# First turns of four layers: the second token half's last two weight blocks multiplied tile by tile

## The chip, the cores and the metric

The kernel runs on one core of one Trainium2 chip. The metric is the device time of one execution in microseconds (us), the median of several runs; lower is better. The engines are PE (TensorE: matmuls and, beside them, loads of its stationary operand), DVE (VectorE), ACT (ScalarE), POOL (GpSimd) and SP (SyncE, here the issuer of most DMAs).

## What is computed

Two models in a row on 512 tokens of width 1024, all in float32. The first is one block: modulated layer norm, a joint projection, two kinds of attention (a forgetting one and a banded one), a gated merge, an output projection, a layer norm, then a feed-forward part. The second puts 16 meta tokens in front (528 tokens) and has two layers: latent attention with a feed-forward part, and a pooling mixer with a feed-forward part. The feed-forward part, which occurs three times, is the one that matters here:

```python
def conv_ffn(h, w_up, conv_w, conv_b, w_down):
    u = h @ w_up                       # 1024 -> 2 * 2816
    up = pad(u, 2 positions in front)
    u = conv_b + sum(conv_w[j] * up[:, j:j + L] for j in range(3))
    gate, val = split(u, 2)
    return (silu(gate) * val) @ w_down
```

The projections named below are up_a (feed-forward part of the first model, 512 tokens), dqkv (the first projection of the latent attention), up_b and up_c (feed-forward parts of the second model's two layers, 528 tokens).

## The kernel before, in words

**Products.** The hardware's fast float32 format keeps fewer bits than float32, so every projection is the sum of three products. A weight block w_raw (128 partitions x 1024) is rounded to w_hi by ACT (`upper`, L1699; the copy itself is L1697), and POOL makes w_lo = w_raw - w_hi (L1513). The layer's input is likewise kept as H_hi (ACT) and H_lo (DVE, L2806 in up_a and dqkv, L2967 in up_b and up_c). `mm3` (L752, matmul at L757) issues w_lo x H_hi, w_hi x H_lo and w_hi x H_hi.

**Turns.** A layer's output is made in turns (11 in each up layer) of four tiles of 128 rows; tile m accumulates in PSUM bank m. The sum runs over eight input tiles of 128 rows, two in each of the turn's four weight blocks (numbers 0 to 3 here; the next turn's are 4 to 7). So a block holds eight 128 x 128 weight tiles: two input tiles by four output tiles. `batch` (L765) runs a turn block by block, and in each block tile by tile.

**First turns in halves.** The layer's input is finished in two token halves, so the first turn of up_a, dqkv, up_b and up_c is run by `head1` (L1195, up_a and dqkv) or `head` (L1282, up_b and up_c) in halves too: first all four blocks for the first half of the tokens, then all four for the second half (256 columns), each by `half_block` (L1081). One half is 4 blocks x 4 tiles x 2 input tiles x 3 products = 96 matmuls. `h_wait` lets PE wait for each input tile of the half as it is first read.

**Signals.** `full` counts finished output tiles 0 to 2 of a turn; it is told as each gets its last product in block 3. `w_used` counts used-up weight blocks; it starts at 4 (the ring has four slots) and is told at the end of each block, in a halved turn in the second half. Tile 3 is told by the last block's w_used. `free[m]` is told when bank m has been read out; PE waits for it before the next turn's first product of tile m (`begin`, L761).

**ACT's program.** ACT works strictly through its own list. In `stage` (L1716) the rounding of coming blocks stands ahead of the reading out of the turn: in the first turn of an up layer, `upper` for blocks 5 and 6 (block 4 is done earlier), then `take` (L1987), then `upper` for block 7. `upper` of block n waits at L1706 until w_used has reached n + 1, that is until block n - 4 has been used up. `take` waits for tile m (`full`, or w_used for tile 3), writes scaled PSUM to `work` (L1994) for the four tiles, then does the silus (L2001) and rounds the products to mid_hi. DVE adds the two other taps of the convolution from PSUM (L2861): first tap of tile 0, first tap of tile 1, second tap of tile 0 (which tells free[0]), second tap of tile 1, and the same for tiles 2 and 3. In up_a and up_b blocks 0 to 3 have a place of their own (up_w_hi and up_w_lo in the trace), but the wait at L1706 for blocks 4 and up is the same.

In dqkv nothing of `take` exists: DVE copies the tiles out (L3061), while ACT rounds blocks 4 to 7 and then squares the copies (L2201) for a norm whose sums PE makes at L815 after block 4. POOL's list follows ACT's roundings (it waits for each), and SP loads a raw block into a slot once POOL has split the one before (`load_w` waits for w_lo_ok).

Of the kernel before, what the change touches and what calls it, by code (L numbers as in the profile page):

```python
# [20 lines left out]
S2 = S1 + META  # L21
# [14 lines left out]
RING = 4  # L36
# [17 lines left out]
BLK0, _n = {}, 0  # L54
# [72 lines left out]
COL2 = 512 - HALF2  # L127
# [26 lines left out]
def program(nc, xT, meta, stream, ada, vecs, consts, rel, rope, yT):  # L154
    with ExitStack() as ctx:
        def sb(name, cols, dt=F32):
            return ctx.enter_context(nc.sbuf_tensor(name, [P, cols], dt))
# [7 lines left out]
        def sem(name):  # L165
            return ctx.enter_context(nc.semaphore(name))
# [4 lines left out]
        w_hi = sb("w_hi", RING * BLK, F32R)  # L171
        w_lo = sb("w_lo", RING * BLK, F32R)
# [59 lines left out]
        own_room = {"up_a": (up1_w_hi, up1_w_lo), "up_b": (up_w_hi, up_w_lo)}  # L232
        z_all, band_w = region(("z_all", 5 * D, F32), ("band_w", 4 * P, F32))
        (_, bands) = region(("over_mid", 2 * KF * S2, F32), ("bands", 3 * BAND, F32))
        PS = ctx.enter_context(nc.psum_tensor("PS", [P, 4, 2 * 512], F32))
# [5 lines left out]
        w_used = sem("w_used")  # L241
        full = sem("full")
# [53 lines left out]
        def halves(name):  # L296
            return sem(name + "_a"), sem(name + "_b")
# [6 lines left out]
        th_ok, hi_ok, hh_ok = halves("th_ok"), halves("hi_ok"), halves("hh_ok")  # L304
# [13 lines left out]
        def ht(t, k, n=S1):  # L318
            return t[:, k * S2:k * S2 + n]

        def half(s, name=None):
            return max(HALVES[s][0], FIRST.get(name, 0)), HALVES[s][1]
# [17 lines left out]
        def tok1(t, k, s, j):  # L340
            return h1(t, k, s)[:, j * P:(j + 1) * P]
# [21 lines left out]
        def tile1(l, s, k):  # L363

            return 2 * KD * l + KD * s + k + 1
# [6 lines left out]
        def taken1(l, s, i):  # L372

            return (2 + (1 - l)) * s + 6 * l + (i // 2 if l else i - 1)
# [28 lines left out]
        def wait_y1(eng, name, s, k):  # L403

            if k < 4:
                wait_out(eng, name, 0, k, 0)
            elif s == 0:
                eng.wait_ge(y1_a, 4 * NORMS1[name] + k - 3)
            else:
                wait_out(eng, name, 0, k - 4, 1)  # L410
# [56 lines left out]
        def wtile(t, slot, kk, m, cols=4):  # L467
            o = slot * BLK + (kk * cols + m) * P
            return t[:, o:o + P]
# [274 lines left out]
        def _(pe):  # L744
# [7 lines left out]
            def mm3(out, w_h, w_l, x_h, x_l, cuts, start, stop):  # L752

                last = None
                for i, (w, x) in enumerate(((w_l, x_h), (w_h, x_l), (w_h, x_h))):
                    for a, b, c0 in cuts:
                        last = pe.matmul(out[:, c0 + a:c0 + b], w, x[:, a:b], start=start and i == 0,  # L757
                                         stop=stop and i == 2)
                return last

            def begin(name, batch, i, g):  # L761

                pe.wait_ge(free[(BATCH[name][batch][2] + i) % 4], free_before(name, batch, i, g) + 1)
# [55 lines left out]
            def hx(T):  # L819
                return lambda k: (ht(H_hi, k, T), ht(H_lo, k, T))  # L820
# [212 lines left out]
            with pe.Fori(0, 2) as g:  # L1033

                for b in range(4):
                    slot = (BLK0["v"] + b) % RING
                    pe.wait_ge(w_lo_ok, g * 4 + (BLK0["v"] + b + 1 + RING))
                    for t in range(4):
                        if b == 0:
                            begin("v", 0, t, g)  # L1040
                        for k in range(2):
                            kt = b * 2 + k
                            wr = slice(slot * BLK + k * 512, slot * BLK + k * 512 + 512)
                            hs = slice(kt * S2 + t * P, kt * S2 + t * P + P)
                            for j, (l, r) in enumerate(((H_lo, w_hi), (H_hi, w_lo), (H_hi, w_hi))):
                                last = pe.matmul(PS[:, t, 0:512], l[:, hs], r[:, wr],  # L1046
                                                 start=kt == 0 and j == 0, stop=kt == 7 and j == 2)
# [30 lines left out]
            def w_ready(n):  # L1078
                pe.wait_ge(w_lo_ok, n + 1 + RING)

            def half_block(name, b, s, rows, k0, x, start, stop, begin_tile=None, told=0, teller=None, h_wait=None,  # L1081
# [20 lines left out]
                        aside(m)  # L1102
                return last

            def sums_y(name, s, k0, k1):

                l = NORMS1[name]
                for k in range(k0, k1):
                    if k == 0:
                        wait_y1(pe, name, s, 4)  # L1110
                    wait_y1(pe, name, s, k)
                    for j in range(2):
                        o, w = 512 * s + WIDE1 * j, 64 * l + 8 * k
                        last = pe.matmul(PS[:, 0, o:o + WIDE1], tok1(X, k, s, j), lnw[:, w:w + WIDE1],  # L1114
                                         start=k == 0 and j == 0, stop=k == KD - 1, skip_group_check=True)
                if k1 == KD:
                    last.then_inc(stat1_ok[s], 1)

            def sums_squares(name, s, k0, k1):

                l = NORMS1[name]
                for k in range(k0, k1):
                    pe.wait_ge(sq1_ok, tile1(l, s, k))
                    for j in range(2):
                        o, w = 512 * s + 2 * WIDE1 + WIDE1 * j, 64 * l + 8 * k + 4
                        last = pe.matmul(PS[:, 0, o:o + WIDE1], tok1(sqx, k, s, j), lnw[:, w:w + WIDE1],  # L1126
                                         start=False, stop=k == KD - 1, skip_group_check=True)
                if k1 == KD:
                    last.then_inc(stat1_ok[s], 1)

            def spread(name, s, i):

                l = NORMS1[name]
                pe.wait_ge(dg1_ok, 2 * value1(l, s, i))
                pe.matmul(spread1(i, s), ones[:, :], diag1(i, s), start=True, stop=True).then_inc(row1_ok, 1)
# [6 lines left out]
            def spread_last(name, s):  # L1142
                if name == "out":
                    spread(name, s, 3)
                spread(name, s, 4)
# [49 lines left out]
            def head1(name, before, x, cuts=None):  # L1195

                l = NORMS1[before]

                def beside(b, m):
                    if b == 1 and m == 3:  # L1200
                        sums_squares(before, 1, 0, 4)
                    elif b == 2 and m == 1:
                        sums_squares(before, 1, 4, KD)
                    elif b == 3 and m == 2:
                        spread(before, 1, 2)
                for s in range(2):
                    def begin_tile(m):
                        pe.wait_ge(rc1_ok, taken1(l, s, 4))
                        if s:
                            begin(name, 0, m, 0)  # L1210

                    def h_wait(k):
                        pe.wait_ge(hh1_ok, tile1(l, s, k))
                    for b in range(4):
                        last = half_block(name, b, s, 2, 2 * b, x, b == 0, b == 3,
                                          begin_tile=begin_tile if b == 0 else None, told=3 * (s == 1 and b == 3),
                                          teller=full, h_wait=h_wait, cuts=None if cuts is None else [cuts[s]],
                                          aside=None if s else (lambda m: beside(b, m)))
                        if s:
                            last.then_inc(w_used, 1)  # L1220
                    if s == 0:
                        spread_last(before, 1)

# [57 lines left out]

            def head(name, before, s, h_base):  # L1282

                for b in range(4):
                    def begin_tile(m):
                        if s == 0:
                            bank_free(before, m, 0)
                        else:
                            begin(name, 0, m, 0)

                    def h_wait(k):
                        pe.wait_ge(hh_ok[s], h_base + k + 1)
                    last = half_block(name, b, s, 2, 2 * b, hx(S2), b == 0, b == 3,
                                      begin_tile=begin_tile if b == 0 else None, told=3 * (s == 1 and b == 3),
                                      teller=full, h_wait=h_wait)
                    if s == 0 and b == 2:
                        sum_x_squares(before, 1)
                    if s:
                        last.then_inc(w_used, 1)

            def pool_rows(i, k):

# [118 lines left out]
            for g in range(2):  # L1421
                for b in range(4):
# [6 lines left out]
                    for j in range(2):  # L1429
                        m = (2 * b + j) % 4  # L1430
# [4 lines left out]
                        for k in range(3):  # L1435

                            pe.wait_ge(h_ok, KD + k + 1)
                            xh, xl = cx(0)(k)
                            last = mm3(PS[:, m, :], wtile(w_hi, slot, k, j, 2), wtile(w_lo, slot, k, j, 2),
                                       xh, xl, spans(S2), k == 0, k == 2)  # L1440
                        last.then_inc(full if j == 0 else w_used, 1)
            pe.wait_ge(h_ok, KD + 5)
            for b in range(2):
                slot = (BLK0["uk"] + b) % RING
                pe.wait_ge(w_lo_ok, BLK0["uk"] + b + 1 + RING)
                for m in range(4):
                    begin("uk", b, m, 0)
                    for k in range(2):
                        xh, xl = cx(3)(k)
                        last = mm3(PS[:, m, :], wtile(w_hi, slot, k, m), wtile(w_lo, slot, k, m),  # L1450
                                   xh, xl, spans(S2), k == 0, k == 1)
# [3 lines left out]
            for b in range(2):  # L1455
                slot = (BLK0["uv"] + b) % RING
                pe.wait_ge(w_lo_ok, BLK0["uv"] + b + 1 + RING)
                for t in range(5):
                    begin("uv", b, t, 0)
                    t0 = KEYS2[t][0]  # L1460
                    for k in range(2):
                        wr = slice(slot * BLK + k * 512, slot * BLK + k * 512 + 512)
                        cs = slice((3 + k) * S2 + t0, (3 + k) * S2 + t0 + P)
                        for j, (l, r) in enumerate(((c_lo, w_hi), (c_hi, w_lo), (c_hi, w_hi))):
                            last = pe.matmul(PS[:, t % 4, 0:512], l[:, cs], r[:, wr],  # L1465
                                             start=k == 0 and j == 0, stop=k == 1 and j == 2)
# [1835 lines left out]
```

## Time and profile before

| | us |
|---|---|
| median of three runs | 2075.13 (2072.96 to 2076.39) |
| the profiled execution | 2074.31 |
| its span | 2072.5 |
| PE busy with matmuls | 2001.7 (97% of the span) |
| DVE busy | 863.9 (42%) |
| ACT busy | 836.6 (40%) |
| POOL busy | 837.1 (40%) |

The span runs from the first to the last instruction that the hardware profiler recorded; the execution's own time is a little longer. All windows and starts below are in us from the span's start. PE's busy share counts a matmul until its modelled end, and the shares of the others are averages over stages that differ. TensorE has two clock levels, 1.2 and 2.4 GHz; the profile gives the granted clock as a share of the higher one.

### The profile page before, as it was taken

What the parts mean: (1) busy time and instruction counts of PE and PEld (TensorE: products, weight loads), DVE (VectorE), ACT (ScalarE), POOL (GpSimd) and SP (SyncE); (2) the same over time, 40 slices, a digit from 0 to 9 for tenths busy, and PEclk for the clock granted to TensorE, in tenths of its full rate; (3) what the DMA queues carried; (4) which work ended last, traced back from release to release, by engine and by line L of the source; (5) the groups of instructions that cost most, each with busy time, mean ns of one, the idle gap of its engine ahead of it and who ended that gap; (6) DMA issues with size and microseconds to landing.
All of it is one profiled execution on the core that took longest, in us unless ns stands there. A gap on an engine that the chain in (4) does not pass through costs nothing.

```text
span 2072.5 us, 35722 instructions
## 1 busy us (share of the span) xinstructions
PE 2001.7 (97%) x13502; PEld 1807.8 (87%) x13506; DVE 863.9 (42%) x1607; ACT 836.6 (40%) x1347; POOL 837.1 (40%) x512
## 2 busy tenths in 40 slices
PE   7999999998999999989999989999999989999997
PEld 5887888888877778979777889999999879999997
DVE  6874540127443340166477274333400663343103
ACT  3124432334544342245577444433422553444322
POOL 1446424450534444324555523444443234434441
PEclk9999999999999999999999999999999999999999
DMA  9742002330322323213200212222232112222321
GB/s 361 278 144 92 17 16 92 96 116 12 102 91 82 102 97 105 72 54 111 72 1 1 67 36 91 81 97 94 84 101 82 62 32 101 91 91 81 112 92 51
DMA packets 54957, 184.47 MB, mean 89 GB/s; under 512 B 6992, under 2 KB 10320, under 8 KB 54864
## 3 DMA queue, kind: packets, MB, share of 16 engines
q1 hardware_dynamic: 53024, 180.97, 26.0%
q10 hardware_dynamic: 1840, 2.19, 0.3%
q8 instruction: 68, 1.11, 0.2%
q14 instruction: 25, 0.20, 0.0%
HBM read 181.03 MB, written 2.10 MB: 88 GB/s over the span
## 4 chain that ended last, share of the span: by engine, by line
PE 87%; DVE 8%; issue 2%; ACT 2%; POOL 1%; DMA 1%; DVEq 0%; ACTq 0%; SPq 0%; POOLq 0%
PE PS L757 70%; PE PS L1046 2%; PE PS L874 2%; PE PS L953 2%; PE PS L838 1%; DVE ada_acc L2396 1%; PE PS L922 1%; DVE work L2861 1%; PE PS L1002 1%; PE PS L865 1%; DVE work L2945 1%; PE PS L1114 1%; PE PS L1126 1%; PE PS L1465 1%; DVE work L2625 1%
## 5 line engine op out<-in xcount | busy, mean ns | idle before, releaser
L1513 POOL TENSOR_TENSOR w_lo<-w_raw,w_hi 128x1024 fp32r<-128x1024 f32 x263 | 637.5, 2430 | 946.8 <-ACT w_hi L1697 946.5
L1697 ACT ACTIVATE w_hi<-w_raw 128x1024 fp32r<-128x1024 f32 (+2 forms) x303 | 291.6, 981 | 715.8 <-PE PS L757 661.4
L757 PE MATMUL PS<-H_hi,w_lo 128*128 128x272 f32 (+3 forms) x2024 | 541.0, 320 | 16.7 <-DVE H_lo L2806 5.6
L757 PE MATMUL PS<-H_lo,w_hi 128*128 128x272 f32 (+3 forms) x2024 | 534.9, 317 | 0.0
L757 PE MATMUL PS<-H_hi,w_hi 128*128 128x272 f32 (+3 forms) x2024 | 533.9, 316 | 0.0
L757 PEld LDWEIGHTS PS<-H_hi,w_lo 128*128 128x128 f32 x2024 | 337.6, 189 | 54.3 <-DVE work L2861 12.9
L2861 DVE SCALAR_TENSOR_TENSOR work<-PS,vec,work 128x512 f32<-128x512 f32 (+4 forms) x264 | 186.9, 751 | 442.9 <-ACT work L1994 433.3
L757 PEld LDWEIGHTS PS<-H_hi,w_hi 128*128 128x128 f32 x2024 | 338.4, 190 | 25.8
L757 PEld LDWEIGHTS PS<-H_lo,w_hi 128*128 128x128 f32 x2024 | 338.1, 190 | 24.7
L757 PE MATMUL PS<-mid_hi,w_lo 128*128 128x256 f32 (+2 forms) x968 | 228.3, 293 | 0.0
L757 PE MATMUL PS<-mid_hi,w_hi 128*128 128x256 f32 (+2 forms) x968 | 226.9, 292 | 0.0
L757 PE MATMUL PS<-mid_lo,w_hi 128*128 128x256 f32 (+2 forms) x968 | 226.6, 292 | 0.0
L757 PEld LDWEIGHTS PS<-mid_hi,w_lo 128*128 128x128 f32 x968 | 158.1, 188 | 4.6 <-issue 0.3
L757 PEld LDWEIGHTS PS<-mid_hi,w_hi 128*128 128x128 f32 x968 | 158.2, 188 | 3.9
L757 PEld LDWEIGHTS PS<-mid_lo,w_hi 128*128 128x128 f32 x968 | 158.0, 188 | 4.0
L1994 ACT ACTIVATE work<-PS,vec 128x512 f32<-128x512 f32 (+1 forms) x132 | 102.5, 784 | 73.3 <-PE PS L757 73.3
L2929 DVE TENSOR_SCALAR work<-PS 128x256 f32<-128x256 f32 (+1 forms) x12 | 5.2, 430 | 132.8 <-ACT work L1810 132.8
L953 PE MATMUL PS<-PT,V 128*128 128x272 f32 (+1 forms) x192 | 54.8, 383 | 5.2 <-DVE work L2625 4.3
L2001 ACT ACTIVATE work<-work 128x512 f32<-128x512 f32 (+1 forms) x66 | 41.7, 632 | 45.0 <-DVE work L2861 45.0
L2396 DVE SCALAR_TENSOR_TENSOR ada_acc<-ada_w,cond,ada_acc 128x1024 f32<-128x1024 f32 x32 | 57.4, 1794 | 1.4
L2921 DVE TENSOR_TENSOR RS<-work 128x528 f32<-128x528 f32 (+1 forms) x3 | 2.1, 703 | 134.1 <-ACT work L1778 134.1
L1522 POOL TENSOR_TENSOR w_lo<-w_raw,w_hi 128x256 fp32r<-128x256 f32 x32 | 24.2, 794 | 74.4 <-ACT w_hi L1697 74.4
(369 smaller groups left out, 2961.0 us busy)
## 6 DMA issues: line engine op xcount, KB each, us to landing
w_raw<-stream SPq DMA_DIRECT2D x289, 512.0 KB, 3.3
ada_w<-ada SPq DMA_DIRECT2D x48, 512.0 KB, 5.4
X<-xT SPq DMA_DIRECT2D x8, 256.0 KB, 5.4
yT<-X SPq DMA_DIRECT2D x16, 128.0 KB, 1.7
rel_raw<-rel ACTq DMA_DIRECT2D x4, 256.0 KB, 2.8
vec<-vecs ACTq DMA_DIRECT2D x1, 390.0 KB, 3.7
sin_t<-rope ACTq DMA_DIRECT2D x1, 264.0 KB, 2.8
cos_t<-rope ACTq DMA_DIRECT2D x1, 132.0 KB, 2.5
```

What stands on the lines that cost most here:

```text
L757: last = pe.matmul(out[:, c0 + a:c0 + b], w, x[:, a:b], start=start and i == 0, stop=stop and i == 2)
L838: pe.matmul(scores1(n, par)[:, 0:w], l[rows, qs], r[rows, 0:w], start=j == 0, stop=False, skip_group_check=True)
L874: last = pe.matmul(o_psum1(par), pt_part1(n, par)[:, j * QB:(j + 1) * QB], v_head1(p, par, j), start=j == 0, stop=j == i, skip_group_check ...
L953: return pe.matmul(o_psum2(par, late)[:, a - a0:b - a0], v_weights2(p, par, j), pt2(par, j, a, b), start=j == 0, stop=stop, skip_group_che ...
L1046: last = pe.matmul(PS[:, t, 0:512], l[:, hs], r[:, wr], start=kt == 0 and j == 0, stop=kt == 7 and j == 2)
L1513: gp.tensor_tensor(w_lo[:, o], w_raw[:, o], w_hi[:, o].bitcast(F32), ALU.subtract)\
L1522: ins = gp.tensor_tensor(w_lo[:, o], w_raw[:, o], w_hi[:, o].bitcast(F32), ALU.subtract)
L1697: return act_.activation(out, in_, ACT.Copy, scale=scale)
L1994: act_.activation(ht(work, m, T)[:, a:], u(m)[:, a:], ACT.Identity, bias=v1("conv", g * 16 + (c + 3)), scale=v1("conv", g * 16 + (c + 2)))\
L2001: act_.activation(y, y, ACT.Silu).then_inc(s_ok, 1)
L2396: ins = v.scalar_tensor_tensor(a, w, cond[:, k:k + 1], a, ALU.mult, ALU.add)
L2861: ins = v.scalar_tensor_tensor(y[:, b:], u[:, b - s:T - s], w, y[:, b:], ALU.mult, ALU.add)
```

## The change

In the second token half, blocks 0 and 1 are run as before, block by block. Blocks 2 and 3 are run by the new `last_pair`: it waits for both blocks first, then takes output tile 0 through block 2 and block 3, then tile 1, and so on. `full` is told after each of tiles 0 to 2. The two w_used signals are both told in tile 3: that of block 2 when tile 3 has had its products of block 2, that of block 3 at the very end. The input tiles 4 to 7 are waited for in tile 0. The first half is unchanged, and so are the lists of ACT, DVE, POOL and SP.

```diff
--- before.py
+++ after.py
@@ -1102,6 +1102,29 @@
                         aside(m)
                 return last
 
+            def last_pair(name, s, k0, x, h_wait, cuts=None):
+
+                h_w, l_w, at = [], [], []
+                for b in (2, 3):
+                    h, l = own_room[name] if name in own_room else (w_hi, w_lo)
+                    h_w.append(h)
+                    l_w.append(l)
+                    at.append((BLK0[name] + b) % RING)
+                    w_ready(BLK0[name] + b)
+                for m in range(4):
+                    for i in range(2):
+                        for k in range(2):
+                            kt = k0 + 2 * i + k
+                            if m == 0:
+                                h_wait(kt)
+                            xh, xl = x(kt)
+                            last = mm3(PS[:, m, :], wtile(h_w[i], at[i], k, m), wtile(l_w[i], at[i], k, m), xh, xl,
+                                       [(*half(s, name), COL2)] if cuts is None else cuts, False, i == 1 and k == 1)
+                        if m == 3:
+                            last.then_inc(w_used, 1)
+                    if m < 3:
+                        last.then_inc(full, 1)
+
             def sums_y(name, s, k0, k1):
 
                 l = NORMS1[name]
@@ -1211,13 +1234,15 @@
 
                     def h_wait(k):
                         pe.wait_ge(hh1_ok, tile1(l, s, k))
-                    for b in range(4):
+                    for b in range(2 if s else 4):
                         last = half_block(name, b, s, 2, 2 * b, x, b == 0, b == 3,
-                                          begin_tile=begin_tile if b == 0 else None, told=3 * (s == 1 and b == 3),
-                                          teller=full, h_wait=h_wait, cuts=None if cuts is None else [cuts[s]],
+                                          begin_tile=begin_tile if b == 0 else None,
+                                          h_wait=h_wait, cuts=None if cuts is None else [cuts[s]],
                                           aside=None if s else (lambda m: beside(b, m)))
                         if s:
                             last.then_inc(w_used, 1)
+                    if s:
+                        last_pair(name, s, 4, x, h_wait, None if cuts is None else [cuts[s]])
                     if s == 0:
                         spread_last(before, 1)
 
@@ -1281,22 +1306,24 @@
 
             def head(name, before, s, h_base):
 
-                for b in range(4):
+                def h_wait(k):
+                    pe.wait_ge(hh_ok[s], h_base + k + 1)
+
+                for b in range(2 if s else 4):
                     def begin_tile(m):
                         if s == 0:
                             bank_free(before, m, 0)
                         else:
                             begin(name, 0, m, 0)
 
-                    def h_wait(k):
-                        pe.wait_ge(hh_ok[s], h_base + k + 1)
                     last = half_block(name, b, s, 2, 2 * b, hx(S2), b == 0, b == 3,
-                                      begin_tile=begin_tile if b == 0 else None, told=3 * (s == 1 and b == 3),
-                                      teller=full, h_wait=h_wait)
+                                      begin_tile=begin_tile if b == 0 else None, h_wait=h_wait)
                     if s == 0 and b == 2:
                         sum_x_squares(before, 1)
                     if s:
                         last.then_inc(w_used, 1)
+                if s:
+                    last_pair(name, s, 4, hx(S2), h_wait)
 
             def pool_rows(i, k):
```

## Rows read from the trace of the kernel before

**Rows 1.** The page: the span, and part 4, the chain that ended last.
```profile
span 2072.5 us, 35722 instructions
...
PE 87%; DVE 8%; issue 2%; ACT 2%; POOL 1%; DMA 1%; DVEq 0%; ACTq 0%; SPq 0%; POOLq 0%
```

**Rows 2.** Waits of PE, whole run: total us, times, longest us.
```profile
PE PS L757 <- DVE H_lo L2806: 9.3, 7, 2.9
PE PS L757 <- DVE H_lo L2967: 8.7, 10, 3.2
...
PE PS L757 <- DVE work L2861: 4.4, 3, 1.6
```

**Rows 3.** Timeline of PE, second turns of up_a, up_b, up_c: start us, us, [idle before].
```profile
527.11 0.51 PE L757 MATMUL PS<-H_hi,w_lo 128*128 128x512 f32 x1 [1.29 <-DVE work L2861]
...
1243.51 0.51 PE L757 MATMUL PS<-H_hi,w_lo 128*128 128x272 f32 x2 [1.60 <-DVE work L2861]
...
1699.71 0.50 PE L757 MATMUL PS<-H_hi,w_lo 128*128 128x258 f32 x2 [1.54 <-DVE work L2861]
```

**Rows 4.** Timeline of ACT, then the chain: up_a, end of the first turn.
```profile
520.27 1.04 ACT L1697 ACTIVATE w_hi<-w_raw 128x1024 fp32r<-128x1024 f32 x1
523.09 1.06 ACT L1697 ACTIVATE w_hi<-w_raw 128x1024 fp32r<-128x1024 f32 x1 [1.78 <-PE PS L757]
524.06 2.77 ACT L1994 ACTIVATE work<-PS,vec 128x512 f32<-128x512 f32 x4
...
524.86 1.43 DVE work L2861 x2
...
526.31 0.76 DVE work L2861
```

**Rows 5.** Timeline of ACT: up_b, end of the first turn.
```profile
1239.19 1.06 ACT L1697 ACTIVATE w_hi<-w_raw 128x1024 fp32r<-128x1024 f32 x1 [1.76 <-PE PS L757]
```

**Rows 6.** Timeline of DVE and POOL: input tiles 6 and 7 in up_a, up_b, up_c.
```profile
519.45 1.79 DVE L2806 TENSOR_TENSOR H_lo<-work,H_hi 128x256 fp32r<-128x256 f32 x1 [1.49 <-ACT H_hi L1697]
...
521.17 0.41 DVE L2806 TENSOR_TENSOR H_lo<-work,H_hi 128x256 fp32r<-128x256 f32 x1
...
1234.95 2.43 DVE L2967 TENSOR_TENSOR H_lo<-work,H_hi 128x256 fp32r<-128x256 f32 x1 [0.35 <-ACT H_hi L1697]
...
1234.69 2.41 POOL L1513 TENSOR_TENSOR w_lo<-w_raw,w_hi 128x1024 fp32r<-128x1024 f32 x1 [9.87 <-ACT w_hi L1697]
...
1691.21 2.43 DVE L2967 TENSOR_TENSOR H_lo<-work,H_hi 128x256 fp32r<-128x256 f32 x1 [0.35 <-ACT H_hi L1697]
```

**Rows 7.** Windows of PE: us, us busy (instructions), granted clock, DMA share, GB/s.
```profile
513.40:516.80 3.40, 3.40 (x18) 0.50 0.00 0
...
896.50:902.50 6.00, 6.00 (x26) 0.50 0.27 87
...
957.30:959.30 2.00, 0.00 (x1) 1.00 0.00 0
...
1663.30:1666.50 3.20, 0.04 (x1) 1.00 0.00 0
...
1243.50:1250.00 6.50, 6.49 (x53) 1.00 0.22 81
```

**Rows 8.** dqkv: timelines of DVE, PE and ACT, then the chain.
```profile
925.59 0.42 DVE L2806 TENSOR_TENSOR H_lo<-work,H_hi 128x256 fp32r<-128x256 f32 x1 [0.15 <-ACT H_hi L1697]
...
932.54 0.28 PE L757 MATMUL PS<-H_hi,w_hi 128*128 128x256 f32 x1
...
930.10 1.12 ACT L1697 ACTIVATE w_hi<-w_raw 128x288 fp32r<-128x288 f32 x4 [0.67 <-PE PS L757]
932.91 1.12 ACT L1697 ACTIVATE w_hi<-w_raw 128x288 fp32r<-128x288 f32 x4 [1.69 <-PE PS L757]
933.95 1.70 ACT L2201 ACTIVATE work<-Q 128x528 f32<-128x528 f32 x3
...
938.69 2.68 PE PS L815 x12
```

## The prediction

> **What bounds the kernel now.** I read the page first: the span and the chain that ended last. PE carries 87% of that chain, most of it one line, L757, the three-product matmul of all projections [rows 1]. A change that only reorders matmuls can gain or lose only where PE stands still, so the next view is who PE waited for. Two kinds of wait touch the changed code: for H_lo, the low half of the layer's input, at the head of a layer (L2806 in up_a and dqkv, L2967 in up_b and up_c), and three waits of 4.4 us together for L2861, the convolution on DVE that frees a PSUM bank [rows 2]. The matmul rows show where these three are: each at the first matmul of the second turn of up_a, up_b and up_c, 1.29, 1.60 and 1.54 us [rows 3]. In no other of the turns between does PE wait, so what is lost at these three places reaches the end of the kernel whole.
>
> Then what holds such a wait up, for up_a. ACT rounds weight block 6 (w_hi) from 523.09 and starts taking tile 0 out of PSUM (L1994) at 524.06; DVE starts its first L2861 at 524.86, and the third of these, from 526.31 on, frees bank 0 and lets PE go on at 527.11 [rows 3, 4]. It is one serial string, and its first link is the rounding of block 6. ACT's program says why: in the first turn `stage` puts `upper` of blocks 5 and 6 ahead of `take`, and `upper` of block 6 waits on w_used (L1706) until block 2 of this turn has been used. ACT idles before it. Between the roundings of blocks 5 and 6, that is between the ends of blocks 1 and 2, lie 2.82 us for 24 matmuls, 0.1175 us each [rows 4]. In up_b block 6 is rounded from 1239.19 on, 4.32 us before PE's restart where up_a has 4.02 [rows 3, 5]; up_c repeats it.
>
> **The change, part by part.** No matmul, weight load or byte is added. In the second half of four first turns the last 48 of 96 matmuls change order: tile 0 over blocks 2 and 3 (12 matmuls), then tiles 1, 2, 3.
>
> (a) Earlier `full`. Tile 0 was complete 18 matmuls before the end and is now 36 before it: 18 x 0.1175 = 2.12 us earlier; tile 1 1.41, tile 2 0.71, tile 3 not. Alone it would start the string earlier.
>
> (b) Later w_used. Block 2 was used up after matmul 72 of the half; now its last matmul is number 90, in tile 3. The signal comes 18 x 0.1175 = **2.12 us later**, and ACT's rounding of block 6 waits for it, with the take of tile 0 queued behind it. ACT cannot use (a): the tile is full, but the engine that takes it stands at the weights. The rounding takes 0.97 us to the next start [rows 4]; from there every link follows as before. Block 3's signal, at the last matmul, does not move.
>
> (c) Earlier need of H_lo. Input tiles 6 and 7 were first read in block 3, 24 matmuls after block 2's start; now after 6 and 9. In up_a the half's last matmul starts at 527.11 - 1.29 - 0.28 = 525.54, so tile 6 would be read 41 matmuls earlier, at 520.72. H_lo of tile 6 is done at 519.45 + 1.79 = 521.24; with 0.04 us to reach PE the wait is 0.56 us. Tile 7, done at 521.58, is wanted three matmuls later at 521.63 and costs nothing more. In up_b: wanted 1241.63 - 4.82 = 1236.81, done 1237.38, wait 0.61; in up_c wanted 1693.07, done 1693.64, wait 0.61. These pieces are late because they run beside POOL's w_lo: 2.43 us where the next takes 0.41 [rows 6]. Nothing in the change moves them. This wait also delays the signal of (b).
>
> So PE's restart moves by 2.12 + 0.56 = 2.68 us in up_a, 2.73 in up_b, 2.73 in up_c: **8.1 us**. PE's gaps grow by 2.12 each, to 3.41, 3.72 and 3.66 us.
>
> (d) The clock. The granted clock stayed at 1.00 (2.4 GHz) after the gaps of 1.3 to 1.6 us [rows 7]. After the five longer ones later than the kernel's first 50 us, from 2.0 (957.30) to 3.2 us (1663.30), it stood at 0.50 (1.2 GHz) for 3.4 us each time, once for 6.0 us of work [rows 7]; the shortest and the longest gap and two of the five stretches stand there. Half clock costs half the stretch: 1.7 us three times, about 1.5 where PE also waited, 3.0 once; the mean is 1.9. The new gaps are longer than all five, so I take 1.9 each, **5.7 us**. Bounds: 0 (as after the 1.6 us gap, the nearest that kept the clock) and 3.0 each, 9 us. PE is what bounds the turn after, so nothing hides this. The Trainium skill (TensorE: Matmul & The Clock Gate, HAM oscillation — how this bites in real kernels) warns of gaps longer than any of the five rows here. By it, strictly read, the 2.0 us gap should have kept the clock, which the trace denies, and up_a's new gap would be borderline: the sum would be about 1.9 us less.
>
> (e) dqkv has no such `take`. ACT rounds blocks 6 and 7 from 930.10 and 932.91 and then squares the outputs from 933.95; PE starts its sums over the squares only after the next 48 full-width matmuls and ends them 2.68 us after 938.69 [rows 8]. Block 6's rounding moves by 2.1 to about 932.2; it holds back block 7's by about 0.3, and the squares by as much, to be done by 936 and covered by over 2 us of those matmuls; without that cover 0.3 us. H_lo of tile 7 is done at 926.01, and block 2 starts at 932.54 - 5.52 = 927.02 [rows 8], so (c) costs nothing here. DVE's copies of tiles 0 to 2 begin earlier, the last ends as now. 0 us. The queues behind in the three up layers: POOL's w_lo of block 6 and SP's load into the slot that it frees also move 2.7 us, but PE wants block 6 only 48 matmuls of double width after the restart (over 11 us) and the load a turn later; 0, and at most the same 2.7 us if that cover were gone.
>
> (f) w_ready of blocks 2 and 3 at the start of the pair: both were multiplied in the first half, 0.
>
> **Sum**: 8.1 + 5.7 + 0 = 13.8 us. The profiled execution took 2074.31 us (span 2072.5), 0.8 below the median of 2075.13; on the median it gives 2088.9.
>
> **Rivals.**
> 1. *The clock holds* (0.12). For it: gaps up to 1.6 us did no harm. Against: the five rows, all of shorter gaps than the new ones. 8.1 us: 2083.2. With the other end of (d) instead, 17.1 us: 2092.2.
> 2. *The tiles are taken early, as (a) has it* (0.05). If ACT's rounding of block 6 did not stand before the take, the string would start at tile 0's end, matmul 60: the third L2861 would end before the half's end in all three layers, PE would not stop, and the time would fall by 1.29 + 1.60 + 1.54 = 4.4 us less the 1.8 of (c): 2.7 us, 2072.4. It decides from the point where the take no longer waits for w_used of block 2. Against it: ACT's idle time ends at exactly that release, and the take follows 0.97 us later though tile 0 had been told by then [rows 4]. The Trainium skill (TensorE: Matmul & The Clock Gate, section Part 1) calls ACT's queue strictly first in, first out, which speaks against this rival; the rows agree. Without (c), if those H_lo pieces came earlier, it would be 4.4 us, 2070.7.
> 3. *Nothing to be seen* (0.03): gain and loss cancel, for instance if ACT's rounding were overtaken in one layer only. 2075.
> The forecast itself has 0.80.
>
> **How the numbers follow.** About 0.2% (4 us) is what a measurement of this kernel can tell from no change. The forecast and rival 1 are slower by more; rival 2 falls mostly within 4 us, rival 3 wholly. Slower 0.92, same 0.06, faster 0.02. The range reaches from a little under rival 1, 2082.0, to a little over the upper bound of (d), 2093.0.
>
> **What would show it.** In the changed kernel: ACT's w_hi of block 6 some 2.7 us later in each up layer, L1994 right behind it; PE's waits for L2861 grown from 4.4 to about 10.8 us in three; new waits of about 0.6 us for H_lo in the pair; stretches of clock 0.50 at the start of the second turns; dqkv's squares at most 0.3 us later. I am wrong if L1994 of tile 0 starts earlier relative to the half's last matmul than now (rival 2), or if the clock stays at 1.00 after the gaps (rival 1). If a gap is 3.4 us or more and the loss still does not reach the end, the claim that nothing else waits in the turns is wrong.

## The result, and the profile after

| | before | changed |
|---|---|---|
| median of 6 runs, us | 2075.76 | 2088.49 (2087.93 to 2089.94) |
| the profiled execution, us | 2074.31 | 2089.11 |
| its span, us | 2072.5 | 2087.3 |

The ratio is 1.0066, 95% interval 1.0056 to 1.0076: the change makes the kernel 12.7 us slower by the medians. Forecast were 13.8 us more and 2088.9.

The page of the changed kernel, with the lines that answer to [rows 1] and two groups of its part 5. The lines of the program move down by 23 to 27, so that L2888 is the convolution that was L2861, L2021 was L1994, L1724 was L1697, L2833 and L2994 were L2806 and L2967.

```profile
span 2087.3 us, 35722 instructions
...
PE 87%; DVE 8%; issue 2%; ACT 2%; POOL 1%; DVEq 0%; DMA 0%; ACTq 0%; POOLq 0%
...
L757 PE MATMUL PS<-H_hi,w_lo 128*128 128x272 f32 (+3 forms) x2024 | 543.8, 322 | 27.4 <-DVE work L2888 10.8
...
L2888 DVE SCALAR_TENSOR_TENSOR work<-PS,vec,work 128x512 f32<-128x512 f32 (+4 forms) x264 | 186.9, 751 | 456.7 <-ACT work L2021 447.2
```

Nothing was added: PE still carries 87% of a longer chain, and the DVE operation costs as much as ever (186.9 us busy). What has grown is the last figure of the PE line, the idle time that ends with L2888, to 10.8 us. The view of PE's waits (total us, times, longest) gives the same, against 4.4 us in three in [rows 2]:

```profile
PE PS L757 <- DVE work L2888: 10.8, 3, 3.7
PE PS L757 <- DVE H_lo L2833: 9.0, 6, 2.9
PE PS L757 <- DVE H_lo L2994: 8.8, 10, 3.2
```

The timeline of PE in up_a, up_b and up_c, against [rows 3] (idle before in brackets):

```profile
521.82 0.39 PE L757 MATMUL PS<-H_hi,up_w_lo 128*128 128x256 f32 x1 [0.45 <-DVE H_lo L2833]
...
526.77 0.28 PE L757 MATMUL PS<-H_hi,up_w_hi 128*128 128x256 f32 x1
530.45 0.80 PE L757 MATMUL PS<-H_hi,w_lo 128*128 128x512 f32 x1 [3.40 <-DVE work L2888]
...
1242.60 0.38 PE L757 MATMUL PS<-H_hi,up_w_lo 128*128 128x256 f32 x1 [0.46 <-DVE H_lo L2994]
...
1251.54 0.81 PE L757 MATMUL PS<-H_hi,w_lo 128*128 128x272 f32 x2 [3.71 <-DVE work L2888]
...
1713.18 0.50 PE L757 MATMUL PS<-H_hi,w_lo 128*128 128x258 f32 x2 [3.65 <-DVE work L2888]
```

The three waits for L2888 are 3.40, 3.71 and 3.65 us where they were 1.29, 1.60 and 1.54. In front of each is a new wait of about 0.45 us in the pair (two of the three stand here), for the H_lo of tile 6. The bracket counts from a matmul's modelled end. From start to start 0.73 us lie there, where two neighbours lie 0.12 apart: the real delay is 0.61 us.

The timeline of ACT in up_a and, from 937.13 on, in dqkv, against [rows 4, 8]:

```profile
520.79 1.04 ACT L1724 ACTIVATE w_hi<-w_raw 128x1024 fp32r<-128x1024 f32 x1
526.43 1.06 ACT L1724 ACTIVATE w_hi<-w_raw 128x1024 fp32r<-128x1024 f32 x1 [4.60 <-PE PS L757]
527.40 2.77 ACT L2021 ACTIVATE work<-PS,vec 128x512 f32<-128x512 f32 x4
...
937.13 2.14 ACT L1724 ACTIVATE w_hi<-w_raw 128x288 fp32r<-128x288 f32 x8 [3.91 <-PE PS L757]
939.18 1.70 ACT L2228 ACTIVATE work<-Q 128x528 f32<-128x528 f32 x3
```

Block 5 is rounded as before. Block 6 now follows 5.64 us behind it (2.82 before), and the read of tile 0 (L2021) starts on its heels, 0.97 us later as before. By then even tile 3 was complete: PE's last matmul of the pair had started at 526.77. In dqkv blocks 6 and 7 are rounded in one go and the squares start at 939.18, 4.4 us ahead of PE's sums (943.60); before it was 4.7 (933.95 and 938.69). Nothing waits for them.

Windows of PE after the three gaps (us, us busy, granted clock, DMA share, GB/s), against [rows 7]:

```profile
530.10:533.50 3.40, 3.05 (x7) 0.50 0.50 154
...
1250.30:1257.10 6.80, 5.56 (x25) 0.50 0.24 77
...
1713.20:1714.50 1.30, 1.30 (x11) 1.00 0.66 180
1714.50:1717.90 3.40, 3.40 (x19) 0.50 0.22 86
```

All three gaps were followed by a stretch at 0.50, the 1.2 GHz level. In up_a it had begun in the gap and left 3.0 us of PE's work at half clock, in up_b 5.6 us, in up_c 3.4 us after 1.3 us at full clock. Half of each is lost: 1.5 + 2.8 + 1.7 = 6.0 us in this execution.

The profiled execution's own bill, from starts in the two traces: in up_a, from PE's start on the second half (511.96, now 512.96) to its restart (527.11, now 530.45), 2.34 us more; from there to the restart in up_b (716.40, now 721.09) 4.69; from there to the restart in up_c (456.20, now 461.64) 5.44; from there to the end 1.33. With 1.0 us that lies before all of this, that is the 14.8 us by which these two executions differ; the medians differ by 2.1 us less.

Two things in this bill come from neither the waits nor the three gaps. The 2.34 us of up_a are 0.4 less than the 2.11 of the longer gap and the 0.61 of the H_lo wait. Both kernels have a stretch at 0.50 at the head of this half. Before, it began 1.4 us after PE's start there and had 3.40 us of work in it [rows 7]; in the changed kernel it began with PE's start, and its first 1.1 us (512.96 to 514.06) hold three matmuls and a short wait that together took as long before (511.96 to 513.06), so less work was slowed. And the clock differed after gaps that the change does not touch: after 2.01 us behind dqkv it fell in the kernel before and not in the changed one, after 1.87 us at the head of up_b it was the other way round:

```profile
1208.30:1210.20 1.90, 0.04 (x1) 1.00 0.00 0
1210.20:1217.00 6.80, 6.25 (x45) 1.00 0.00 0
```

in the kernel before, and in the changed kernel

```profile
1213.40:1215.30 1.90, 0.08 (x1) 1.00 0.00 0
...
1216.00:1219.40 3.40, 3.25 (x14) 0.52 0.00 0
```

Over the four such gaps between the restarts of up_a and up_b, PE's work at half clock is about 13 us in both. That they cancel in this pair of executions is luck.

### The profile page after: what moved, and what is told of

The parts are those of the page before. It is cut to its first block, busy times and chain, and to the rows that moved or that the text cites. A ratio compares the mean times of both kernels' runs of the same rounds, so it can differ in the third digit from the quotient of the medians.

```text
span 2087.3 us, 35722 instructions
## 1 busy us (share of the span) xinstructions
PE 2009.0 (96%) x13506; PEld 1813.8 (87%) x13506; DVE 868.9 (42%) x1607; ACT 836.7 (40%) x1347; POOL 835.9 (40%) x512
## 4 chain that ended last, share of the span: by engine, by line
PE 87%; DVE 8%; issue 2%; ACT 2%; POOL 1%; DVEq 0%; DMA 0%; ACTq 0%; POOLq 0%
PE PS L757 71%; PE PS L1046 2%; PE PS L874 2%; PE PS L953 2%; PE PS L838 1%; PE PS L922 1%; DVE work L2888 1%; PE PS L865 1%; DVE work L2972 1%; PE PS L1137 1%; PE PS L1002 1%; PE PS L1149 1%; PE PS L1492 1%; DVE H_lo L2994 1%; DVE work L2652 1%
## 5 line engine op out<-in xcount | busy, mean ns | idle before, releaser
L1724 ACT ACTIVATE w_hi<-w_raw 128x1024 fp32r<-128x1024 f32 (+2 forms) x303 | 291.9, 981 | 732.5 <-PE PS L757 676.4
L757 PE MATMUL PS<-H_hi,w_lo 128*128 128x272 f32 (+3 forms) x2024 | 543.8, 322 | 27.4 <-DVE work L2888 10.8
L2888 DVE SCALAR_TENSOR_TENSOR work<-PS,vec,work 128x512 f32<-128x512 f32 (+4 forms) x264 | 186.9, 751 | 456.7 <-ACT work L2021 447.2
L2021 ACT ACTIVATE work<-PS,vec 128x512 f32<-128x512 f32 (+1 forms) x132 | 102.4, 783 | 73.3 <-PE PS L757 73.3
```

The costliest lines, as they stand in the source:

```text
L1724: return act_.activation(out, in_, ACT.Copy, scale=scale)
L2021: act_.activation(ht(work, m, T)[:, a:], u(m)[:, a:], ACT.Identity, bias=v1("conv", g * 16 + (c + 3)), scale=v1("conv", g * 16 + (c + 2)))\
L2888: ins = v.scalar_tensor_tensor(y[:, b:], u[:, b - s:T - s], w, y[:, b:], ALU.mult, ALU.add)
```

## The experiments

Each experiment was run 5 to 11 times and is compared with 15 to 32 executions of the kernel before on the same chip. Differences are of medians; the ratios with their 95% intervals follow.

**1. ACT's list: the read ahead of block 6's rounding.** The four reads of the first turn no longer stand behind `upper` of block 6:

```diff
                             .then_inc(y_ok, 1)
+                    if isinstance(g, int):
+                        upper(up, RING + 2)
                     for j in range(2):
...
-                    stage(up, 0, lambda bi: take(0, psum2), 1)
+                    stage(up, 0, lambda bi: take(0, psum2), 1, (RING + 2,))
```

(`stage` leaves out the blocks in its last argument; the same for up_a.)

> The changed kernel, with ACT's rounding of weight block 6 moved behind the four reads of tiles 0 to 3 in the first turns of the three up layers; PE's order as changed. Theory (the late w_used of block 2 holds the read of tile 0 behind it in ACT's list): the read starts when tile 0 is told, PE's three waits for L2888 (10.8 us) go to about 0, the clock stays up, the H_lo waits of 0.5 us remain: 2.7 us under the kernel before, near 2073. Rival (the tile order itself costs, through matmuls or H_lo): stays over 2083.

Measured: 2072.59 against 2074.99, ratio 0.9987 (0.9978 to 0.9996): 2.4 us faster than before, and some 15 us faster than the changed kernel with the same order on PE. ACT in up_a:

```profile
523.33 0.78 ACT L2022 ACTIVATE work<-PS,vec 128x512 f32<-128x512 f32 x1 [0.92 <-PE PS L757]
...
527.52 0.78 ACT L2022 ACTIVATE work<-PS,vec 128x512 f32<-128x512 f32 x1 [0.64 <-PE PS L757]
528.20 1.05 ACT L1724 ACTIVATE w_hi<-w_raw 128x1024 fp32r<-128x1024 f32 x1
```

and PE there, at the change of turns:

```profile
527.20 0.28 PE L757 MATMUL PS<-H_hi,up_w_hi 128*128 128x256 f32 x1
527.32 0.40 PE L757 MATMUL PS<-H_hi,w_lo 128*128 128x512 f32 x1
```

ACT reads tile 0 at 523.33, 3.9 us before PE's last matmul of the pair; reads of 0.78 us follow one by one as tiles finish, and PE goes from the last matmul of the turn to the first of the next in 0.12 us. No wait of PE for the convolution is left in the list of its waits. Apart from the waits for H_lo (0.30, 0.46 and 0.45 us here, experiment 6) the tile order costs nothing by itself; the reads stood behind the wrong thing.

**2. The clock: the gap half filled.** PE multiplies into a free corner of PSUM behind tile 3; the rest of the program is the changed one.

```diff
+                        if m == 3 and i == 1 and name != "dqkv":
+                            for _ in range(18):
+                                last = pe.matmul(PS[:, 3, 768:1024], H_hi[:, META:META + P], H_hi[:, META:META + 256],
+                                                 start=True, stop=True, skip_group_check=True)
                         if m == 3:
                             last.then_inc(w_used, 1)
```

> The changed kernel with 18 matmuls of 256 columns that nobody reads behind tile 3 of the pair in the up layers, so that PE is busy for 2.1 us of each gap. Theory (5.7 us of the loss is the clock at half after the gaps): PE restarts at the same time after the pair, the gaps are about 1.3 to 1.6 us, the granted clock stays 1.00 after them, and the time falls to 8.1 us over the kernel before, near 2084. Rival (no cost of the clock, the waits are all): the same as the changed kernel, 2088.5.

Measured: 2084.11 against 2074.99, ratio 1.0041 (1.0027 to 1.0055), 9.1 us slower. Windows around the three places:

```profile
529.80:531.00 1.20, 0.00 (x0) 1.00 0.00 0
531.00:538.00 7.00, 6.98 (x30) 1.00 0.21 75
...
1251.40:1258.00 6.60, 6.59 (x54) 1.00 0.26 82
...
1710.50:1717.00 6.50, 6.47 (x54) 1.00 0.27 83
```

At these three places PE is idle for no longer than 1.55 us, and the clock stays at 1.00. Against the changed kernel's 12.7 us, 3.6 us are gone by medians though PE restarts no earlier. That is the price of the clock as this run shows it, under the 5.7 expected; by the ratios (1.0066, 1.0041) it is 5.2. The intervals are wide enough for both, and for the 5.7 too. The other 8 to 9 us are waits.

**3. Half the dose.** Only tile 0 runs ahead; block 2 is used up after 30 of the pair's 48 matmuls.

```diff
-                for m in range(4):
-                    for i in range(2):
...
+                for m, i in ((0, 0), (0, 1), (1, 0), (2, 0), (3, 0), (1, 1), (2, 1), (3, 1)):
```

> The pair in the order tile 0 over blocks 2 and 3, then tiles 1 to 3 of block 2, then tiles 1 to 3 of block 3: block 2 is used up after 30 of the 48 matmuls, not 42 (changed kernel) or 24 (before). Theory: ACT's rounding of block 6 comes 6 matmuls (0.7 us) plus the H_lo wait of 0.6 later than before, so 1.3 us a layer, 3.9 in all, 2079.7 if the clock holds; the gaps are 2.0, 2.3 and 2.2 us, and where the clock falls after them 1.9 us more each, up to 2085.4. Rival (the loss does not follow the release of block 2): the same as the changed kernel.

Measured: 2081.52 against 2074.99, ratio 1.0028 (1.0016 to 1.0039), 6.5 us slower. Windows of the gaps and of what followed:

```profile
526.00:528.00 2.00, 0.04 (x1) 1.00 0.05 18
528.00:535.00 7.00, 6.96 (x30) 1.00 0.24 75
1244.20:1246.50 2.30, 0.03 (x1) 1.00 0.06 23
...
1246.80:1250.20 3.40, 3.40 (x17) 0.50 0.45 154
...
1703.80:1706.10 2.30, 0.06 (x2) 1.00 0.04 14
...
1707.60:1711.00 3.40, 3.40 (x18) 0.50 0.14 58
```

and the third gap in PE's timeline:

```profile
1706.09 0.51 PE L757 MATMUL PS<-H_hi,w_lo 128*128 128x258 f32 x2 [2.24 <-DVE work L2887]
```

The gaps are 2.00, 2.30 and 2.24 us, as worked out from the release of block 2. After the first the clock held, after the other two it stood at 0.50 for 3.4 us. The 3.9 us of waits that were expected (the gaps grew by 2.1 in all, the rest is the waits for H_lo) and 2 x 1.7 us of clock make 7.3; 6.5 were measured. The loss follows the release, not the fact of a new order.

**4. dqkv alone.** The pair only where name is "dqkv".

> The pair in dqkv alone, the three up layers as before. Theory: no change, 2075.8. Rival (the move of the squares behind block 7's rounding reaches the end): 0.3 us or more over the kernel before.

Measured: 2074.81 against 2074.99, ratio 1.0003 (0.9994 to 1.0012). ACT there rounds blocks 6 and 7 in one go, as in the changed kernel:

```profile
931.26 2.14 ACT L1722 ACTIVATE w_hi<-w_raw 128x288 fp32r<-128x288 f32 x8 [2.81 <-PE PS L757]
933.30 1.70 ACT L2226 ACTIVATE work<-Q 128x528 f32<-128x528 f32 x3
```

The squares start 4.4 us ahead of PE's sums (937.73) here too, and the time does not move: the interval runs from 1.2 us faster to 2.5 us slower. So dqkv has at most a small part of the 12.7 us, and the three up layers have the rest.

**5. The signal alone.** ACT's list as changed, but w_used of block 2 told early where no ring slot hangs on it:

```diff
-                        if m == 3:
+                        if (m, i) == ((0, 0) if name in own_room else (3, 0)) or (m, i) == (3, 1):
                             last.then_inc(w_used, 1)
```

> The changed kernel, where w_used for block 2 is told after tile 0 has had block 2 (matmul 6 of the pair) in up_a and up_b, whose first four blocks do not lie in the ring that it guards; up_c keeps the late signal. ACT's list is as changed. Theory (it is this signal, not the order of ACT's list as such): in up_a and up_b PE does not wait for L2888 and gains 0.7 and 1.0 us on the kernel before; up_c loses 2.7 plus 1.9 for the clock; in sum 2.9 us over the kernel before, 2078.7. Rival (the order of PE's work costs by itself): within 2 us of the changed kernel.

Measured: 2076.53 against 2075.13, ratio 1.0010 (1.0001 to 1.0019), 1.4 us slower, 11 us faster than the changed kernel. Of PE's three waits for the convolution one is left, that of up_c:

```profile
PE PS L757 <- DVE work L2888: 3.6, 1, 3.6
```

One signal moved by 36 matmuls in two layers takes away most of the loss. It came out 1.5 us better than forecast; the gap at H_lo in up_a was 0.23 us in its profile (0.45 in the changed kernel), and the rest may be scatter, which no run settles: the interval is 4 us wide.

**6. The early need of H_lo alone.** The kernel before with two waits:

```diff
+                        if m == 1 and b == 2 and s and name[:3] == "up_":
+                            h_wait(k0 + 2 + k)
```

> The kernel before with nothing but two waits moved in the second halves of the up layers: input tile 6 waited for after 6 matmuls of block 2, tile 7 after 9, as the changed kernel does. Theory: 0.5 to 0.6 us a layer, 1.7 us in all, 2077.5, with PE's gaps before the second turns unchanged. Rival (the wait is taken back later because ACT and DVE catch up in it): 2075.8.

Measured: 2077.24 against 2075.13, ratio 1.0013 (1.0004 to 1.0022), 2.1 us slower. PE in up_b:

```profile
1237.06 0.39 PE L757 MATMUL PS<-H_hi,up_w_lo 128*128 128x256 f32 x1 [0.45 <-DVE H_lo L2969]
...
1243.87 0.51 PE L757 MATMUL PS<-H_hi,w_lo 128*128 128x272 f32 x2 [1.55 <-DVE work L2863]
```

The wait in the pair is there with its 0.45 us, and the gap before the second turn is 1.55 us for 1.60 before: the delay is passed on nearly whole. In up_a and up_c it is the same, with waits of 0.45 and 0.46 us and gaps of 1.29 and 1.55.

**7. ACT's list alone.** The edit of experiment 1 on the kernel before.

> The kernel before, block by block, with only ACT's list changed as in the first experiment. Theory: tile 0 is told 0.35 us before ACT took it, so 0.35 us a layer and 1.0 in all, 2074.7. Rival (it is ACT's list alone that pays, and the order of tiles adds nothing): as low as the first experiment.

Measured: 2074.42 against 2075.13, ratio 0.9996 (0.9987 to 1.0005), inside the noise. PE's three waits for the convolution fell from 4.4 to 3.7 us in all: block by block there is little for ACT to take earlier.

**8. Tiles, ACT's list and POOL together.** Experiment 1, and POOL waits with w_lo of block 4 until the half's last H_lo:

```diff
             lower_ahead("up_a")
+            gp.wait_ge(hh1_ok, tile1(0, 1, KD - 1))
             lower_blocks(BLK0["up_a"] + RING, BLK0["dqkv"])
...
             add_x("wo", 1)
+            gp.wait_ge(hh_ok[1], KD)
...
             add_x("pool", 1)
+            gp.wait_ge(hh_ok[1], 2 * KD)
```

> The first experiment, and POOL begins its w_lo of block 4 in the up layers only when the last H_lo of the second half is done, so that DVE's last two H_lo do not run beside it. Theory: the H_lo waits of the pair (0.45 to 0.6 us each) go too, 4.4 us under the kernel before, 2071.4. Rival (H_lo of tile 6 is slow by itself): the same as the first experiment.

Measured: **2070.16** against 2075.13, ratio 0.9978 (0.9969 to 0.9988), 5.0 us faster than the kernel before. DVE's last two H_lo of up_b:

```profile
1234.17 0.76 DVE L3000 TENSOR_TENSOR H_lo<-work,H_hi 128x256 fp32r<-128x256 f32 x2 [0.35 <-ACT H_hi L1727]
```

and PE (us, us busy) across the end of the first turn in the three layers:

```profile
524.50:531.00 6.50, 6.50 (x37) 1.00 0.46 161
1240.00:1246.00 6.00, 6.00 (x50) 1.00 0.30 97
1695.00:1701.00 6.00, 6.00 (x52) 1.00 0.25 89
```

The two pieces take 0.76 us together, where the first alone took 2.43 beside POOL [rows 6], and PE is busy without a break. POOL's part in the gain is not clear of the noise: experiment 1 without it was 2.4 us faster than the kernel before, and the two intervals overlap.

**9. The same without the tile order.** ACT's list and POOL's later start on the kernel before.

> The kernel before, block by block, with ACT's list of the first experiment and POOL's later start of block 4. Theory: block by block neither H_lo piece is waited for in block 3, so the later start of POOL gives nothing here, and the time is that of the kernel before with ACT's list alone, about 2074.4; then the 5 us of the run with tiles, ACT's list and POOL together need the tile order. Rival (POOL's later start gains by itself): near 2071.

Measured: 2073.82 against 2075.03, ratio 0.9998 (0.9989 to 1.0007). PE's waits for the convolution are as in experiment 7:

```profile
PE PS L757 <- DVE work L2867: 3.7, 3, 1.4
```

So the gain of experiment 8 needs the tile order of the change: with it the interval ends at 0.9988, without it it begins at 0.9989.

**10. POOL's later start on the changed kernel.**

> The changed kernel with only POOL's later start of block 4. Theory: the H_lo waits of the pair go (1.8 us at most, less where a low clock at the head of up_a already hides them), the three waits for L2888 stay at 10.8 us with their low clock: about 2087. Rival (the H_lo wait is what makes the gaps long): the waits for L2888 shrink too.

Measured: 2085.26 against 2075.03, ratio 1.0052 (1.0038 to 1.0065), 10.2 us slower. The waits for L2891 (the same convolution) stay at 10.8 us in three. The first of them, and PE after each:

```profile
530.18 0.50 PE L757 MATMUL PS<-H_hi,w_lo 128*128 128x512 f32 x1 [3.40 <-DVE work L2891]
...
530.20:535.00 4.80, 4.80 (x21) 1.00 0.32 109
1248.70:1255.60 6.90, 5.38 (x24) 0.51 0.24 76
1709.50:1716.40 6.90, 5.38 (x25) 0.51 0.22 76
```

The H_lo waits are gone from the pair and the gaps are 3.40, 3.71 and 3.65 us as in the changed kernel: the H_lo wait moved the string, and did not lengthen the gaps. 2.5 us less than the changed kernel's 12.7, where 1.8 were expected at most; the intervals overlap. The five executions differ by 4.3 us, and their mean granted clock goes with it: the longest, 2087.92 us, which is the profiled one, had 0.985, the shortest, 2083.66, had 0.988.

## Why the prediction was right, point by point

The forecast was 2088.9 for a measured 2088.49, with its mechanism borne out. That the two lie within 0.4 us is partly luck: the sum of 13.8 us was put on 2075.13, the median of three runs, where the median of six is 2075.76. The change itself measured 12.7 us, 1.1 less than the sum.

(a) and (b), the earlier `full` that ACT cannot use and the later w_used: right. The read of tile 0 starts 0.97 us behind block 6's rounding in both traces, and the gaps grew by 2.11, 2.11 and 2.11 us for 2.12 forecast. Experiments 1 and 5 take the dependence away from either side, by ACT's order in all three layers and by PE's signal in up_a and up_b, and there the gaps vanish; experiment 3 halves the shift and the gaps follow.

(c), the early need of H_lo, 1.8 us: right in size, with a delay of 0.61 us in up_b and up_c for 0.61 forecast. Alone it measured 2.1 us (experiment 6), and that POOL's w_lo is what makes the pieces late shows in experiments 8 and 10, where the waits go with POOL's later start. In up_a it depends on the clock: the second half begins there after a gap of 2.6 us, and where half clock lasts until some 6 us after PE's restart, as in the profiles of experiments 1 and 5 (3.4 us in the changed kernel), PE reaches tile 6 later and the gap is only 0.30 and 0.23 us.

(d), the clock, 5.7 us: the right mechanism. The profile shows 6.0 us lost, experiment 2 puts 3.6 (medians) to 5.2 us (ratios) on it. The medians' 12.7 for a sum of 13.8 fits a term somewhat smaller than I had it. Experiment 10 shows how that can be: after the gap of 3.40 us in up_a the clock stayed at 1.00, so to charge every gap that is longer than the five rows was too strict. How often this happens in the changed kernel's own executions is not shown. The lower bound was also misread: the gap nearest to the new ones that kept the clock was not that of 1.6 us but one of 1.87 us at the head of up_b (window 1208.30:1210.20 above), and the bound of 0 rests on that one instead. The Trainium skill's longer bound (TensorE: Matmul & The Clock Gate, HAM oscillation — how this bites in real kernels), weighed in the prediction, describes that one gap better than my reading of the rows; the fall after the same 3.40 us in the changed kernel lies at its edge, and the falls after 2.24 and 2.30 us in experiment 3 go against it again.

(e) and (f), dqkv and the queues behind: right, 0 (experiment 4), the squares 0.3 us later against PE's sums.

Rival 2, the tiles taken early, had its point of decision where it was put. Experiment 1 is that rival made true: 2.4 us faster for 2.7 worked out, and with (c) taken away too 5.0 for 4.4. That nothing else waits in the turns was right as well: in the bill above all that PE lost at the three places is in the end time.

## What to carry to other kernels

When work is reordered so that an output is finished sooner, list every signal that the reordering makes later, and find what each engine does in its list between that signal and the output: an engine that works its list in order cannot take the early output while it waits for the late signal. Here one release that moved by 18 matmuls cost 2.1 us three times, and where such a gap was followed by half clock for 3.4 us, 1.7 us more each time. The same reordering paid 5 us once the reads stood ahead of that wait and POOL kept off DVE while the last inputs were made, so a slower result can be the right order with a list not yet fitted to it.

## What the runs showed that I had not expected

The length of a gap alone does not say whether the clock falls. After 1.87 us it held in the kernel before and fell in the changed one, at the same place. After 2.01 us the kernel before fell to 0.50 and after 2.00 us experiment 3 did not; after 2.24 and 2.30 us it fell; after 3.40 us it fell in the changed kernel and not in experiment 10, which has the same gap at the same place. The stretch at half clock, too, differs after gaps of the same length at the same place: in up_c, after 3.65 us, it was 3.4 us in the changed kernel and 6.8 us in experiment 10, of which 5.4 us held work of PE. So the clock's share is a term to give as a range, and a single profile's share is one draw from it.
